# First FFN's norm with sums in four column groups and a reciprocal of 128x64; the FFN's first two products interleaved

## What is computed

```
x = x + g1 * (o @ w_out[l])
h2 = modulate(rmsnorm(x, norm_ffn[l]), sh2, sc2)
x = x + g2 * conv_ffn(h2, w_up[l], conv_w[l], conv_b[l], w_down[l], rows)

def conv_ffn(h, w_up, taps, conv_b, w_down, rows):
    a, g = jnp.split(h @ w_up, 2, axis=-1)
    ...
    return (a * jax.nn.gelu(gc, approximate=False)) @ w_down
```

## Time and profile before

| | |
|---|---|
| median of three executions | 945.72 us (944.54 to 946.80) |
| the profiled execution's own time | 945.89 us |
| its span | 943.9 us |
| PE busy | 922.8 us, 98% of the span, 8610 instructions |
| DVE busy | 731.0 us, 77% |
| ACT busy | 482.3 us, 51% |
| POOL busy | 15.4 us, 2% |
| granted TensorE clock, mean | 1.00 |

### The profile page before, as it was taken

How to read it: one execution, slowest core, us unless ns; L and a number is a source line. 1 busy time by engine, 2 the same in 40 slices (tenths; PEclk the granted TensorE clock), 3 DMA queues, 4 the chain that set the end, 5 groups by cost and what they waited for, 6 DMA issues and landing times.

```text
span 943.9 us, 19838 instructions
## 1 busy us (share of the span) xinstructions
PE 922.8 (98%) x8610; PEld 866.9 (92%) x8610; DVE 731.0 (77%) x1088; ACT 482.3 (51%) x586; POOL 15.4 (2%) x35
## 2 busy tenths in 40 slices
PE   6999999999999999999999999999999999999997
PEld 4688999999989999999999999999999999999986
DVE  3689998869898989867957985555786997878863
ACT  3453535655546566448664853234636444443363
POOL 0000000002000000000200000000000000000000
PEclk9999999999999999999999999999999999999999
DMA  9997353673457757525653334433355555556531
GB/s 339 344 300 256 112 179 115 217 250 112 145 176 249 234 189 259 179 91 179 218 190 148 129 132 154 163 107 126 132 175 193 183 183 180 181 192 207 179 134 44
DMA packets 114021, 171.67 MB, mean 182 GB/s; under 512 B 3256, under 2 KB 96720, under 8 KB 109840
## 3 DMA queue, kind: packets, MB, share of 16 engines
q1 hardware_dynamic: 111680, 165.63, 52.0%
q0 software_dynamic: 1056, 2.36, 0.8%
q10 hardware_dynamic: 1200, 2.43, 0.7%
HBM read 169.34 MB, written 1.06 MB: 181 GB/s over the span
## 4 chain that ended last, share of the span: by engine, by line
PE 81%; DVE 9%; ACT 5%; DMA 3%; issue 1%; ACTq 0%; DVEq 0%
PE bank L1201 24%; PE bank L1203 23%; PE bank L1202 23%; DVE wlo L641 3%; ACT whi L632 2%; DMA raw<-in_w_in_dram 2%; DVE arena L2382 1%; PE bank L1240 1%; PE bank L1254 1%; DMA arena<-in_table_dram 1%; PE bank L1804 1%; ACT hhi L679 1%; DVE raw L2117 1%; DVE arena L2471 1%; PE bank L1722 1%
## 5 line engine op out<-in xcount | busy, mean ns | idle before, releaser
L1201 PE MATMUL bank<-hhi,whi 128*128 128x256 f32 (+1 forms) x1744 | 506.5, 290 | 5.6 <-DVE arena L2471 1.8
L1203 PE MATMUL bank<-hhi,wlo 128*128 128x256 f32 (+1 forms) x1744 | 500.2, 287 | 0.0
L1202 PE MATMUL bank<-hlo,whi 128*128 128x256 f32 (+1 forms) x1744 | 500.1, 287 | 0.0
L641 DVE TENSOR_TENSOR wlo<-raw,whi 128x2048 fp32r<-128x2048 f32 x131 | 299.4, 2287 | 101.0 <-ACT whi L632 83.0
L1201 PEld LDWEIGHTS bank<-hhi,whi 128*128 128x128 f32 x1744 | 334.0, 192 | 14.6 <-issue 9.8
L1202 PEld LDWEIGHTS bank<-hlo,whi 128*128 128x128 f32 x1744 | 334.2, 192 | 3.8 <-issue 1.0
L1203 PEld LDWEIGHTS bank<-hhi,wlo 128*128 128x128 f32 x1744 | 334.1, 192 | 2.6
L632 ACT ACTIVATE whi<-raw 128x2048 fp32r<-128x2048 f32 x131 | 250.3, 1913 | 131.4 <-PE bank L1203 123.8
L1201 PE MATMUL bank<-whi,hhi 128*128 128x256 f32 (+1 forms) x256 | 87.3, 341 | 0.8 <-ACT arena L1161 0.8
L1202 PE MATMUL bank<-wlo,hhi 128*128 128x256 f32 (+1 forms) x256 | 86.1, 336 | 0.0
L1203 PE MATMUL bank<-whi,hlo 128*128 128x256 f32 (+1 forms) x256 | 86.1, 336 | 0.0
(11 more groups left out here) (380 smaller groups left out, 795.5 us busy)
## 6 DMA issues: line engine op xcount, KB each, us to landing
raw<-in_w_up_dram SPq DMA_DIRECT2D x44, 1024.0 KB, 5.1
raw<-in_w_in_tiles_dram SPq DMA_DIRECT2D x32, 1024.0 KB, 4.8
raw<-in_w_down_dram SPq DMA_DIRECT2D x22, 1024.0 KB, 5.0
raw<-in_w_ada_dram SPq DMA_DIRECT2D x19, 1024.0 KB, 5.9
raw<-in_w_in_dram SPq DMA_DIRECT2D x14, 1024.0 KB, 5.6
raw<-in_w_branch_dram SPq DMA_DIRECT2D x6, 1024.0 KB, 5.1
arena<-in_w_ada_dram SPq DMA_DIRECT2D x10, 512.0 KB, 9.5
raw<-in_w_out_dram SPq DMA_DIRECT2D x4, 1024.0 KB, 5.5
```

Source lines behind the costliest of these rows:

```text
L641: dve.tensor_tensor(wlo[:, g % RING, :], raw[:, n % RING, :], whi[:, g % RING, :].bitcast(F32), ALU.subtract).then_inc(w_lo, 1)
L1201: pe.matmul(o, wh, ah, start=start, stop=False, **kw)
L1202: pe.matmul(o, wh, al, start=False, stop=False, **kw)
L1203: return pe.matmul(o, wl, ah, start=False, stop=stop, **kw)
```

## The change

Four things change, all around the norm of the first FFN.

- The sums of squares: each of the eight feature blocks is multiplied in four token quarters of 64, each with ones of 128x32 and into its own strip of 32 partitions, so that strip q holds the sums of tokens 64q to 64q + 63. ACT's root and DVE's reciprocal then cover 128x64.
- PE spreads the reciprocal again into a new small unit `rt1`: four matmuls, each with one column of the identity (32q) broadcast to 128 columns as weights and `rstd[:, 0:64]` as the moving operand, fill a bank with the four quarters on all partitions. DVE scales from that bank.
- The filler matmuls become two ahead of the spread and four behind it.
- `fg0` and `fa0` are interleaved: k = 0 and 1 of `fg0`, k = 0 and 1 of `fa0`, the rest of `fg0`, the rest of `fa0`.

The ring's new unit is handed back by the memset of `weigh`, whose own signal falls away, so the later wait on `weigh_ready` counts one less.

```diff
--- before.py
+++ after.py
@@ -237,7 +237,7 @@
                 ("do1", "act")]
     m_units = [(n, "act") for n in ("kfT0", "kfT1", "wsT", "kbT0", "kbT1", "hf", "hb")]
     m_units += [("oA", "act"), ("oB", "act"), ("on", "act"), ("z0", "dve"), ("z1", "dve"), ("rn0", "dve"), ("rn1", "dve"),
-                ("sum1", "act"), ("A5", "dve"), ("sum2", "dve"), ("sum3", "act"), ("norm1", "act"), ("smg", "act"), ("sm", "dve"), ("colT", "dve")]
+                ("sum1", "act"), ("rt1", "dve"), ("A5", "dve"), ("sum2", "dve"), ("sum3", "act"), ("norm1", "act"), ("smg", "act"), ("sm", "dve"), ("colT", "dve")]
     m_units += [(n, "act") for n in ("lk0", "lk1", "sfq0", "sfq1", "sfk0", "sfk1", "rq")]
     m_units += [("pT", "dve"), ("on2", "act"), ("on3", "act"), ("row4", "act"), ("sum4", "act")] + [(f"hT{n}", "dve") for n in range(4)]
 
@@ -490,7 +490,7 @@
         var_ready, rstd_ready, weigh_ready = sem("var_ready"), sem("rstd_ready"), sem("weigh_ready")
         diag_ready = sem("diag_ready")
         ada_scaled = sem("ada_scaled")
-        heads_rstd = sem("heads_rstd")
+        heads_rstd, quarters_rstd = sem("heads_rstd"), sem("quarters_rstd")
         masks_loaded, masks_ready = sem("masks_loaded"), sem("masks_ready")
         ada_late, keys_summed, vn_used = sem("ada_late"), sem("keys_summed"), sem("vn_used")
         fk_zero, fk_rows, rq_ready, fgain_ready = (sem(n) for n in ("fk_zero", "fk_rows", "rq_ready", "fgain_ready"))
@@ -848,7 +848,7 @@
                         if g == 2:
                             act.activation(table_kept, eps, ACT.Sqrt)
             squares(lambda c: (g_empty["dve"], g_emptied(g_no(f"wo{c}"))[1]), G["wo0"])
-            norm_std("sum1", T, D)
+            norm_std("sum1", 64, D)
             norm_hi(HT[:, 0:KT * T], 2, shift=lambda k, n: mod[:, 24 + k, 0:1])
             split_hi(act, G["wo3"] + RING)
 
@@ -1534,13 +1534,41 @@
             for c in range(2, 4):
                 gemm(f"wo{c}", 512, lo=T)
             ada_unit(4)
-            sum_squares("sum1", 0, T)
-            keep_clock(bank[4], 10)
+            o = m_open("sum1")
+            for k in range(KT):
+                if k % 2 == 0:
+                    pe.wait_ge(sq_ready, k // 2 + 1)
+                for q in range(4):
+                    at = T * k + 64 * q
+                    ins = pe.matmul(o[STRIPS[q], 0:64], ones[:, 0:32], SQ[:, at:at + 64], start=k == 0,
+                                    stop=k == KT - 1, skip_group_check=True)
+            ins.then_inc(m_full, 1)
+            keep_clock(bank[4], 2)
+            o = m_open("rt1")
+            pe.wait_ge(quarters_rstd, 1)
+            for q in range(4):
+                ins = pe.matmul(o[:, 64 * q:64 * q + 64], ident[:, 32 * q:32 * q + 1].broadcast_to([P, P]),
+                                rstd[:, 0:64], start=True, stop=True)
+            ins.then_inc(m_full, 1)
+            keep_clock(bank[4], 4)
+
+            def first_up(name, ks):
+
+                wh, wl = w_parts(name, KT)
+                bk = g_open(name) if ks[0] == 0 else g_bank(name)
+                for k in ks:
+                    h_wait(8, k, True)
+                    for nb in range(2):
+                        ws = [x[:, k, P * nb:P * (nb + 1)] for x in (wh, wl)]
+                        ins = product(bk[:, T * nb:T * (nb + 1)], ws, acts(T, k), k == 0 and nb == 0, k == KT - 1,
+                                      skip_group_check=True)
+                if ks[-1] == KT - 1:
+                    ins.then_inc(g_full, 1)
 
             def both_sums(g):
 
                 o = m_bank("sum2")
-                pe.wait_ge(weigh_ready, 2)
+                pe.wait_ge(weigh_ready, 1)
                 pe.wait_ge(sq_ready, 4 + g + 1)
                 for k in (2 * g, 2 * g + 1):
                     for t in range(2):
@@ -1572,10 +1600,13 @@
 
             for j in range(FFT // 2):
                 if j == 0:
-                    gemm_first("fg0", T, 8)
+                    first_up("fg0", range(2))
+                    first_up("fa0", range(2))
+                    first_up("fg0", range(2, KT))
+                    first_up("fa0", range(2, KT))
                 else:
                     gemm(f"fg{j}", T)
-                gemm(f"fa{j}", T)
+                    gemm(f"fa{j}", T)
                 if j == 3:
                     pe.wait_ge(*g_done("fg2"))
                     pe.wait_ge(*g_done("fa2"))
@@ -2028,9 +2059,10 @@
             def normalise(ht, g0, w, xs, scale, shift, m_u):
 
                 dve.wait_ge(m_empty["act"], m_emptied(m_no(m_u))[1])
-                link(dve.reciprocal(rstd[:, 0:w], std[:, 0:w]))
+                dve.reciprocal(rstd[:, 0:64], std[:, 0:64]).then_inc(quarters_rstd, 1)
+                dve.wait_ge(m_full, m_no("rt1") + 1)
                 for g in range(4):
-                    scaled(ht, w, xs, scale, g)
+                    scaled(ht, w, xs, scale, g, m_bank("rt1"))
                     if g > 0:
                         low_parts(ht, w, shift, g0, g - 1)
                 low_parts(ht, w, shift, g0, 3)
@@ -2360,7 +2392,7 @@
 
             dve.tensor_tensor(gain2, par("norm_final", 8), par("g_mix", 8), ALU.mult)
             link(dve.tensor_tensor(nf2, par("norm_final", 8), par("norm_final", 8), ALU.mult))
-            dve.memset(weigh[:, :, 0:1], 1.0).then_inc(weigh_ready, 1)
+            dve.memset(weigh[:, :, 0:1], 1.0).then_inc(m_empty["dve"], 1)
             dve.tensor_copy(weigh[:, :, 1:2], nf2.unsqueeze(2)).then_inc(weigh_ready, 1)
 
             def ada_sum(u):
```

## The result

The change makes the kernel slower: 951.23 us (median of 20 runs, 948.02 to 953.65) beside 945.98 for the kernel before (20 runs, 943.67 to 951.8); the ratio is 1.0048, 95% interval 1.0035 to 1.0062. The forecast was 944.5, within 943.3 to 946.7. The profiled execution took 949.64 us, its span is 947.6.

What follows compares the result with a forecast made beforehand. DVE's order of work from fg0's drain to about 279 us was taken as the bound. First product 2.40 us earlier, less 1.12 for interleaving, gave 1.28: 944.61, or 944.5 on the median's scale; range 943.3 to 946.7.

Steps and rivals of the forecast that it cites:

- Sum of squares: PE's sums in the first FFN's norm, in four column groups, were to end 2.25 us earlier.
- Root: ACT's root in the norm, on 128x64 in place of 128x256, was to be 0.14 us shorter.
- Reciprocal: DVE's reciprocal in the norm, on 64 columns in place of 256, was to take 0.55 us, 1.20 less.
- Spread: PE's new step between reciprocal and scaling, eight instructions plus hand-offs, was to cost 1.19 us.
- a factor read from PSUM: DVE's scaling from a PSUM bank: at worst 0.1 us ahead of the first high part, taken as nothing.
- the fast end: Forecast's fast bound: spread at 0.75 us and the sum at its lower bound, gain 1.9 us, time 943.8.
- The interleaving: At the first FFN products, 12 of fa0 inside fg0 were to make fg0's drain 1.12 us later, net.
- DVE's chain from the drain to 279: From fg0's drain to about 279 us, DVE's rigid order of work sets the time; PE has slack.
- Rival 1: PE's eight units, not DVE's order, are the chain, so all 2.40 us arrive: 943.3; 13%.
- rival 2: The sums' column groups run one after another, the sum ends at 212.3, net 1.0 lost: 946.7; 9%.
- Rival 3: The array falls to its lower clock ahead of the first products, 7.2 us longer: 951.6; 5%.
- The rest: Remaining effects (filler from 20 instructions to 12, POOL's loads, DVE's split, semaphore, small ring) were to add no wait.

Runs made afterwards that it cites:

- e4: The kernel before with only the interleaving of fg0 and fa0 added: 946.64 us, ratio 1.001.
- e6: The kernel after with the interleaving undone and 39 tiny matmuls added inside a later PE wait (fourth pair of units): 941.83 us, ratio 0.9967.
- e5: The kernel after, all four fillers kept, with 38 tiny matmuls added inside a later PE wait (fourth pair of units): 945.66 us, ratio 0.9995.
- e7: The kernel after, its four fillers kept, with 152 padding instructions behind them ahead of the first products: 945.63 us, ratio 0.9996.
- e1: The kernel after with its last filler cut from 4 to 2 and 40 tiny strip matmuls added: 945.52 us, ratio 1.001.
- e3: The kernel after with the interleaving undone, the last filler cut to 2 and 42 tiny matmuls behind it: 944.17 us, ratio 0.9993.
- e9: The kernel after with the interleaving undone and nothing padded: 947.47 us, ratio 1.0014.

## Why the prediction was wrong

*The local terms were right*, counted from the fourth square. Sum of squares: the root starts 2.20 earlier (forecast 2.25); 48 matmuls of 64 columns take 0.88, 0.018 each, near the forecast's 0.017. This pace is well under the 0.025 of the rule that the prediction weighed (the Trainium skill, page "TensorE: Matmul & The Clock Gate", section "Wait — 56ns, not 53.3ns?"): the trace differs from it, and decides. Root 0.31 for 0.47: 0.16 (0.14). Reciprocal 0.55 for 1.75: 1.20 (1.20). Spread: from the reciprocal's end to the scaling 1.26, where it was 0.04: 1.22 later (1.19); its eight instructions take the 1.07 that the 2-column row had given. From scaling to first product 2.88 before and after, so that a factor read from PSUM costs nothing. 2.20 + 0.16 + 1.20 - 1.22 = 2.34. One of the bounds does not come out of its own terms: for the spread, eight quarters of 0.23 and twice 0.2 make 0.86, or 1.0 with the hand-off, not 0.75, so the fast end was about 944 and not 943.8. The outcome does not turn on it.

*The interleaving*: 1.14 by e4 and 1.18 between after and e6, forecast 1.12. It is the one of the four edits that loses on balance where it stands; undoing it is worth about 1.1 us.

*DVE's chain from the drain to 279*: held. PE's waits there are 1.3 longer, and with the count set right (e5, e7) 1.1 us of the 1.2 arrive at the kernel's end. Rival 1 (2.40 in full) falls by this, rival 2 by the sum's end.

*Rival 3*, the lower clock at the first products: not in the kernel after, whose granted clock there is 1.00. It came in e1 and e3, at a fifth of the price that I gave it (next section).

*The step that failed is "The rest"*: "The filler goes from 20 instructions to 12, cover for waits only." I priced each added and removed PE instruction by its time where it stands, and not at all for its place in the stream. The sums, spread and filler make that stream 103 instructions longer, and everything behind them, to the kernel's end, sits at another place in its block. Before, no block came late in the second block's bursts; that was a matter of the count, and a near one: there the packets start 2.5 to 3.6 us before PE reaches their block, and in the waits of the slower kernels PE goes on 2.2 to 2.7 us after the packet starts. The count's price was 5.8 us, five times the gain, and no rival of mine held it: the nearest, "slower", had 0.09 and rested on the clock. With it, 945.98 - 1.2 + 5.8 = 950.6, beside the measured 951.23. Could it have been read from the profile of before? The q8 line, the bursts of 128 tiny matmuls under full loads and these thin margins were there, but no gap to warn; a change of PE's count by anything but a multiple of 256 should have been given a bound above of several microseconds, and the range would then have held the result.

**What stays open**: which counts are harmless can't be worked out from these runs. 1, 156, 208, 253 and 255 lose 0 to 0.4, 6 loses 0.8, 52 2.6, 97 to 104 5 to 6; the loads move with the FFN as well, a late block seems to make later ones late, and I found no rule that gives these from the profile of before.

## What to carry to other kernels

An edit changes not only what runs but where every later instruction of that engine sits in its program; where bursts of tiny instructions run beside bulk loads, compare the engine's gaps that have no releaser before and after, far from the edit too. When a kernel gets slower in a stage that was not touched, repeat the old kernel with the new count of instructions (a few idle ones added) before looking for any other reason. Before such an edit is judged, measure it with its count brought near a multiple of 256 away from the old one: here that turned 1.0048 into 0.9996, and with the interleaving dropped into 0.9967.

## What the runs showed of the hardware

The stall for instructions itself: up to 1.5 us in one cut (e9; 1.35 after). In all 21 waits PE goes on 2.2 to 2.7 us after the block's packet starts, with a 1 MB load ahead of the packet or without.

And the clock: e1 and e3 replace four of the eight full-width matmuls ahead of the first products by tiny ones in strips. PE then stands 1.02 us (e1) and 1.19 (e3) before its first product, where it stands 1.13 after the change, so it is about as idle. But the granted clock at the products falls. Windows of 4 us from 0.65 us past the first product's start: e1, then after, then e7, which has all eight and the tiny ones too (columns as above):

```profile
213.50:217.50 4.00, 4.00 (x24) 4.00 (x23) 3.23 (x8) 3.32 (x5) 0.95 (x1) 0.59 0.20 49
```
```profile
214.96:218.96 4.00, 4.00 (x36) 4.00 (x35) 3.23 (x8) 3.31 (x5) 0.96 (x1) 1.00 0.17 45
```
```profile
217.12:221.12 4.00, 4.00 (x36) 4.00 (x35) 3.23 (x8) 3.32 (x5) 0.99 (x2) 1.00 0.18 45
```

A mean of 0.59 (0.57 in e3) is mostly the 1.2 GHz level: 24 products pass in place of 36, and 12 at 0.12 us are the 1.4 that the drain of e1 is late. So the filler was not cover alone, as the prediction had it: with four full-width matmuls fewer, and about as many microseconds of tiny ones in strips in their place, the drain came 1.2 us (e3) and 1.5 us (e1) later. That is one profiled execution of each.
